# Two 128x128 turns moved from TensorE to VectorE and DRAM, taps in other places, the last block by token half

## The chip, the cores and the metric

One core of a Trainium2 chip runs the whole program. The metric is device time in microseconds (us). The kernel before took 2549.4 us, the median of three runs (2548.04 to 2549.49).

## The reference

Two transformer-like blocks over 256 tokens of width 2048, all in float32. What matters here:

```python
# first block, feed-forward (D_FF = 5632)
f = (silu(h @ w_ffn_gate) * (h @ w_ffn_up)) @ w_ffn_down

# second block, mixer: 2048 + 2*4*128 = 3072 convolved channels
proj = rmsnorm(h) @ w_in                  # z, xbc, dt_raw, q, k, v
xbc  = silu(causal_dwconv(xbc, conv_w, conv_b))   # width 4, along the tokens
# then a state-space scan over xbc and dt, gated by z, and
# attention in a window of 128 tokens over q, k, v; both into w_out

# second block, feed-forward, with a causal convolution of width 3 before the gate
# last: h + sigmoid(rmsnorm(h) @ w_ple_gate) * rmsnorm(p @ w_ple_proj)
```

## The kernel before

**Products.** Float32 operands are split into a high part (float32r, by ACT, line 781) and a low part (the rest, by VectorE, line 2157), and every product is three TensorE passes: high x high, high x low, low x high (lines 1475 to 1477, in `tokens`). A phase (`up1`, `down1`, `w_in2`, `up2`, `ple_gate` and so on) is a row of blocks of 512 output columns. A block streams its weights from DRAM in tiles of 512 rows (four slots of `raw`, by SP, `load_tile`); each tile is two halves (four slots of `w_hi` and of `w_lo`). With 2048 inputs a block has eight halves. A weight half may be split only when TensorE has used the half four before it; ACT and VectorE run three halves ahead (`LEAD = 3`). So in the loops of ACT and VectorE the place n of a block stands beside TensorE's half n, and splits half n + 3. What else ACT, VectorE and TensorE have to do is put at places by hand, after the split of that place (TensorE: after the half). Each engine runs its own list in order; semaphores join them.

**Tokens and channels.** Products come out with tokens on the partitions, in the PSUM banks `pair[:, b % 2]`, two blocks in turn. What is needed with channels on the partitions has to be turned.

- *First feed-forward* (`up1`, 22 blocks, half of the columns from the gate, half from the up matrix): at the end of block b ACT takes the SiLU of the gate half (`finish_up1`, line 1123) and VectorE multiplies by the up half into `ff_u` (`product`, line 2610). Beside half 3 of the next block TensorE turns the 2 x 2 squares of 128 x 128 into the PSUM tile `misc` (`turn_hidden`, line 1794), ACT copies them to `hid_hi` (line 1128), VectorE subtracts for `hid_lo` (line 2616). `down1` starts with the last of these. During the first blocks VectorE also sums modulation rows (line 2377), whose 512 KB tiles POOL loads.
- *Convolved channels* (`w_in2`, blocks 6 to 11 of 16, six blocks of 512 channels, `B_XBC` to `B_Z`): at the end of a block ACT evicts it, scaled by the norm, to `xbc_t` (line 1170). Beside half 0 of the next block TensorE turns it back into the bank it came from (`turn_xbc`, eight transposes, line 1950). At place 1 ACT writes the tap of the newest token with the bias into `xbc` (`conv_bias`, line 936, four instructions), and VectorE adds the three older taps, four instructions each, two at each of the places 1 to 6 (`conv_taps`, line 2318). TensorE's next block but one writes the same bank: it waits at its start for all twelve (`pe.wait_ge(c2_tap, 12 * (j - 1))`). The first z block turns the sixth.
- *Attention beside it*: from place 4 of the first convolved block one of 16 pairs of heads every two places. TensorE: values and scores after an even half (lines 1877, 1856, 1857), transposes of the probabilities after an odd one (line 1868). VectorE at each odd place: mask and maxima of one pair (lines 2748 to 2761), inverses and scaling of the pair before (lines 2764 to 2775). ACT: exponentials at even places (lines 1196, 1200), copies at odd ones (1208 before the split, 1233 after it). VectorE's `attention_beside` calls `attention(place)` and then `convolution(place)`.
- *Second feed-forward* (`up2`): the turn goes another way already. ACT evicts with the columns permuted into `ff_t`; SP writes it to DRAM (`keep_up2`) and reads it back (`back_up2`), so that what belongs to one 128 x 128 square is spread over the partitions such that VectorE's turn of 32 x 32 squares (`turn_up2`, line 3001) finishes it, into `misc`, at place 3.

**The end.** `ple_gate` has four blocks. After the last, ACT takes the sigmoid of each token half (line 1439), VectorE multiplies and adds (lines 3053, 3058), and SP stores each half.

Of the kernel before, what the change touches and what calls it, by code (L numbers as in the profile page):

```python
# [87 lines left out]
def two_blocks(nc, d, out):  # L88
# [125 lines left out]
    with ExitStack() as ctx:  # L214
# [84 lines left out]
        ff_u = at("ff_u", F + 90, [P, 2, S])  # L299
        ff_t = at("ff_t", R, [P, 4, T, P])  # L300
# [21 lines left out]
        xbc_t = at("xbc_t", F + 88, [P, T, COLS])  # L322
# [81 lines left out]
        def columns(tile, widths):  # L404
# [40 lines left out]
        ff_sig, ff_prod, ff_turned, h_hi, h_lo, c3_bias, c3_tap, up2_ev, up2_kept, up2_back, up2_turned = (  # L445
            sem(n) for n in ("ff_sig", "ff_prod", "ff_turned", "h_hi", "h_lo", "c3_bias", "c3_tap", "up2_ev", "up2_kept", "up2_back",
                             "up2_turned"))
        qkv_ev, dt_acc, dt_ev, xbc_turned, dt_hi, dt_lo, dt_mm, dt_x, dt_exp, hn_v, hn_s, k_ready, q_ready, qk_turned, qk_ev = (
            sem(n) for n in ("qkv_ev", "dt_acc", "dt_ev", "xbc_turned", "dt_hi", "dt_lo", "dt_mm", "dt_x", "dt_exp", "hn_v", "hn_s", "k_ready", "q_ready",
# [38 lines left out]
        TURN3_AT, CONV3_AT, SILU3_AT = 3, 4, 6  # L488


        TURN_XBC_AT, CONV2_AT, SILU2_AT, LATE_AT = 0, 1, 3, 4
# [30 lines left out]

        end_in, dt_raw, res_ready = sem("end_in"), sem("dt_raw"), sem("res_ready")
# [78 lines left out]
        def _(sp):  # L602
# [85 lines left out]

            def load_up1(b):
                load(up1, b, twin(d["w_ffn_gate"][0], b * (COLS // 2), d["w_ffn_up"][0], b * (COLS // 2)))  # L690
# [9 lines left out]
            load_all(down1, d["w_ffn_down"][0])  # L700
# [4 lines left out]
            for b in range(1, w_in2.blocks):  # L705
                if b == 2:
                    load_late()
                load(w_in2, b, plain(d["w_in_2"][0], bass.ds(w_in2_cols[b], COLS)))
            for b in range(w_out2.blocks):
                load(w_out2, b, plain(d["w_out_2"][0], bass.ds(b * COLS, COLS)))  # L710
            def keep_up2(b):

                sp.wait_ge(up2_ev, b + 1)
                if not isinstance(b, int) or b:
                    sp.wait_ge(up2_back, b * 16)
                sp.dma_start(up2_rows.rearrange("g p n -> p g n"), ff_t.rearrange("p g t q -> p g (t q)")).then_inc(up2_kept, 16)

            def back_up2(b):

                sp.wait_ge(up2_kept, b * 16 + 16)  # L720
                if not isinstance(b, int) or b:
                    sp.wait_ge(up2_turned, b)
                sp.dma_start(ff_back.rearrange("p i t q -> p (i t q)"),
                             up2_rows.rearrange("g (a i) n -> (g a) (i n)", i=4)).then_inc(up2_back, 16)

            def load_up2(b, turn):
                for j in range(up2.tiles):
                    load_tile(up2, b, j, twin(d["w_up_2"][0], b * (COLS // 2), d["w_up_2"][0], b * (COLS // 2) + HC * P))
                    if turn and j == 0:
                        keep_up2(b - 2)  # L730
                    elif turn and j == 1:
                        back_up2(b - 2)
# [5 lines left out]
            for j in range(down2.tiles):  # L738
                load_tile(down2, 0, j, plain(d["w_down_2"][0], bass.ds(0, COLS)))
                if j in (0, up2.tiles):  # L740
                    keep_up2(up2.blocks - 2 + j // up2.tiles)
                elif j in (1, up2.tiles + 1):
                    back_up2(up2.blocks - 2 + j // up2.tiles)
# [24 lines left out]
        def _(act):  # L768
# [298 lines left out]
            def gate2_out():  # L1067

                act.wait_ge(gt_row, XB + 1)
                act.wait_ge(res_ready, XB)  # L1070
                done(run(gt[0:KC, 0:P], misc[0:KC, 2, 0:P], ACT.Copy))
                done.wait()
                act.dma_start(by_chunk(gate_row_kept[0]), gt[0:KC, 0:P]).then_inc(row_ready, 16)
# [42 lines left out]
            def finish_up1(b, c):  # L1116

                if isinstance(b, int) and b == 8:
                    act.wait_ge(ple_landed, PLE_STORED)
                    mod_out(MOD_SUMS.index(9) + 1, JOINT_USED + 1, misc[:, 3, :], rows_late)  # L1120
                if not isinstance(b, int) or b:
                    act.wait_ge(ff_prod, b)
                run(ff_g[:], pair[:, c, :, GATE], ACT.Silu).then_inc(ff_sig, 1)

            def hidden_high(b, c):

                act.wait_ge(ff_turned, b)
                run(flat(hid_hi[:, bass.ds(b * 2 - 2, 2), :]), misc[:, c, :], ACT.Copy).then_inc(h_hi, 1)

            stream(up1, finish_up1, down1, peel=5, evict=hidden_high)  # L1130
            def beside_down1(b, place):
                if b:
                    norm2_beside(b - 1, place)
                elif place == LAST_HIDDEN + 1:
# [123 lines left out]
            for b in range(B_XBC, B_Z):  # L1258
                j = b - B_XBC
                mixer2(b, attention_beside, output)  # L1260
                if j:
                    act.wait_ge(xbc_turned, j)
                evict(xbc_t, b % 2).then_inc(qkv_ev, 1)
# [96 lines left out]
            def conv3_bias(b, c):  # L1360

                act.wait_ge(up2_turned, b)
# [25 lines left out]
            def finish_up2(b, c):  # L1388
# [3 lines left out]
                else:  # L1392
                    act.wait_ge(up2_kept, b * 16)
# [25 lines left out]
            for b in range(ple_gate.blocks):  # L1419
# [13 lines left out]
                act.wait_ge(w_used, ple_gate.end(b))  # L1433
# [4 lines left out]
                for t in range(T):  # L1438
                    ins = run(sig[:, t, :], pair[:, b % 2, t, :], ACT.Sigmoid, scale=scale[:, t:t + 1])
# [5 lines left out]
        def _(pe):  # L1445
# [340 lines left out]
            def turn_hidden(b, c):  # L1786

                pe.wait_ge(ff_prod, b)
                if not isinstance(b, int) or b > 2:

                    pe.wait_ge(h_lo, b - 2)
                for e in range(2):
                    for t in range(T):
                        mm = pe.transpose(misc[:, c, e * S + t * P:e * S + (t + 1) * P], ff_u[:, t, e * P:(e + 1) * P], ident[:])
                mm.then_inc(ff_turned, 1)

            def up1_block(b, c):

                def beside(h):
                    if h == 3 and (not isinstance(b, int) or b):  # L1800
                        turn_hidden(b, 1 - c)
# [24 lines left out]
            def last_hidden_turned(h):  # L1826
                if h == 0:
                    gate2_turn()
                elif h == LAST_HIDDEN:
                    turn_hidden(up1.blocks, 1)  # L1830
# [114 lines left out]
            def turn_xbc(j):  # L1945

                pe.wait_ge(qkv_ev, B_XBC + j)
                for m in range(4):
                    for t in range(T):
                        mm = pe.transpose(pair[:, (B_XBC + j - 1) % 2, m // 2, m % 2 * S + t * P:m % 2 * S + (t + 1) * P],  # L1950
                                          xbc_t[:, t, m * P:(m + 1) * P], ident[:])
                mm.then_inc(xbc_turned, 1)


            for b in range(B_XBC, B_Z):
# [6 lines left out]
                def beside(h):  # L1962
                    if j and h == TURN_XBC_AT:
                        turn_xbc(j)
# [77 lines left out]
            for b in range(B_Z, w_in2.blocks):  # L2042
# [6 lines left out]
                def beside(h):  # L2049
                    if j == 0 and h == TURN_XBC_AT:  # L2050
                        turn_xbc(B_Z - B_XBC)
# [89 lines left out]
            for b in range(ple_gate.blocks):  # L2141
                if b >= 2:
                    pe.wait_ge(gate_sig, b - 1)
                tokens(ple_gate, b, b % 2, normed, embedding if b == 0 else None, normed_yet(4) if b == 0 else None)


        @block.vector
        def _(dve):
# [13 lines left out]
            def stream(ph, finish, nxt, mod_pairs=0, beside=None, evict=None, paced=None):  # L2162
# [12 lines left out]
                def one(b, c, more, mods=False):  # L2175
# [6 lines left out]
                    if not (mods and b == 0):  # L2182
                        split_lo(ph, b, range(ph.lead, ph.halves), beside)
# [420 lines left out]
            def product(b, c):  # L2604

                dve.wait_ge(ff_sig, b + 1)
                if not isinstance(b, int) or b:

                    dve.wait_ge(ff_turned, b)
                dve.tensor_tensor(ff_u[:], ff_g[:], pair[:, c, :, UP], ALU.mult).then_inc(ff_prod, 1)  # L2610
# [8 lines left out]
            stream(up1, product, down1, mod_pairs=4, evict=hidden_low)  # L2619
# [24 lines left out]
            def beside_down1(b, place):  # L2644
                if b:
                    norm2_beside(b - 1, place)
                elif place == LAST_HIDDEN + 1:
                    hidden_low(up1.blocks, 1)
# [198 lines left out]

            def convolution(place):
# [149 lines left out]
            def turn_up2(b, c):  # L2998

                dve.wait_ge(up2_back, b * 16)  # L3000
                dve.transpose(misc[:, 2 * c:2 * c + 2, :].rearrange("p k (e t a i) -> p i t (k e) a", e=2, t=T, i=4),
                              ff_back.rearrange("p i t (m q) -> p i t m q", m=4)).then_inc(up2_turned, 1)
# [103 lines left out]
```

## Time and profile before

| | |
|---|---|
| median of three runs | 2549.4 us |
| the profiled execution | 2547.73 us, span 2546.0 us |
| TensorE busy | 2512.1 us (99%) |
| VectorE busy | 1608.0 us (63%) |
| ACT busy | 1255.5 us (49%) |
| first feed-forward's up blocks | from about 394 to 871 us |
| convolved channels | from about 1240 to 1425 us |
| granted TensorE clock | 0.998 of full |

Times in rows are from the span's start. A timeline row is start, duration, engine, line, operation, output and inputs, count of merged instructions, and in brackets the idle time before it and what ended that. An instruction of TensorE or VectorE overlaps the next one a little, so the distance of two starts tells more of what it costs than its duration.

### The profile page before, as it was taken

The page shows a single profiled execution, that of the slowest core. Times are in us where ns is not written, and L with a number is a line of the kernel's source. Part 1 is how long each engine was busy: PE and PEld are TensorE (multiplying, and loading weights), DVE is VectorE, ACT ScalarE, POOL GpSimd, SP SyncE. Part 2 cuts the span into 40 slices and gives each one's busy share as a digit, 9 for nine tenths or more (in the row PEclk, how much of TensorE's full clock was granted, in tenths as well). Part 3 has the DMA queues.
Part 4 walks back from the last instruction along what each step waited for, and adds up shares of the span by engine and source line. Part 5 has one row for each costly group of instructions (what it writes and reads, how often), then busy time and mean ns, then how long its engine had stood idle before and what let it go on. Part 6 is the DMA issues. An engine that isn't in the chain of part 4 may idle for free.

```text
span 2546.0 us, 32176 instructions
## 1 busy us (share of the span) xinstructions
PE 2512.1 (99%) x12226; PEld 2047.7 (80%) x12226; DVE 1608.0 (63%) x1958; ACT 1255.5 (49%) x1665; POOL 78.6 (3%) x165
## 2 busy tenths in 40 slices
PE   7999999999999999999999999999999999999999
PEld 1688878888888888888888888888888888888887
DVE  1468997764444455565888678446777777744445
ACT  2354454444444444454566656445555555544463
POOL 0012110100000000000000000000000000000000
PEclk9999999999999999999999999999999999999999
DMA  9999998865555556575534555566777777755564
GB/s 385 392 347 388 356 338 286 294 232 188 186 194 182 193 187 198 187 220 167 181 118 134 178 201 166 183 197 217 245 244 239 240 238 237 234 193 184 192 231 132
DMA packets 367708, 579.37 MB, mean 228 GB/s; under 512 B 19520, under 2 KB 213088, under 8 KB 367088
## 3 DMA queue, kind: packets, MB, share of 16 engines
q1 hardware_dynamic: 347088, 504.68, 59.5%
q0 software_dynamic: 19616, 71.34, 7.5%
q10 hardware_dynamic: 896, 1.84, 0.3%
q8 instruction: 75, 1.23, 0.2%
q14 instruction: 33, 0.27, 0.0%
HBM read 563.36 MB, written 14.46 MB: 227 GB/s over the span
## 4 chain that ended last, share of the span: by engine, by line
PE 93%; DMA 3%; DVE 2%; ACT 1%; issue 1%; SPq 0%; POOL 0%; DVEq 0%; ACTq 0%
PE pair L1475 28%; PE pair L1477 27%; PE pair L1476 27%; DMA mod_raw<-in_w_ada 2%; PE pair L1457 1%; PE pair L1458 1%; PE pair L1459 1%; PE misc L1628 1%; DVE w_lo L2157 1%; PE misc L2039 1%; PE misc L1491 1%; PE misc L1877 1%; DMA mod_page<-in_w_ada 0%; PE misc L1868 0%; PE misc L1856 0%
## 5 line engine op out<-in xcount | busy, mean ns | idle before, releaser
L2157 DVE TENSOR_TENSOR w_lo<-raw,w_hi 128x1024 fp32r<-128x1024 f32 x848 | 1015.6, 1203 | 786.0 <-ACT w_hi L781 783.4
L781 ACT ACTIVATE w_hi<-raw 128x1024 fp32r<-128x1024 f32 x848 | 882.4, 1043 | 982.9 <-PE pair L1477 906.6
L1475 PE MATMUL pair<-w_hi,a_hi 128*128 128x512 f32 x2048 | 805.6, 393 | 0.9 <-DVE w_lo L2157 0.7
L1477 PE MATMUL pair<-w_hi,a_lo 128*128 128x512 f32 x2048 | 797.8, 390 | 0.0
L1476 PE MATMUL pair<-w_lo,a_hi 128*128 128x512 f32 x2048 | 797.1, 389 | 0.0
L1475 PEld LDWEIGHTS pair<-w_hi,a_hi 128*128 128x128 f32 x2048 | 384.5, 188 | 83.6 <-issue 2.9
L1477 PEld LDWEIGHTS pair<-w_hi,a_lo 128*128 128x128 f32 x2048 | 384.4, 188 | 81.0
L1476 PEld LDWEIGHTS pair<-w_lo,a_hi 128*128 128x128 f32 x2048 | 384.7, 188 | 77.8 <-issue 0.5
L1475 PE MATMUL pair<-w_hi,hid_hi 128*128 128x512 f32 x704 | 274.6, 390 | 0.0
L1477 PE MATMUL pair<-w_hi,hid_lo 128*128 128x512 f32 x704 | 274.0, 389 | 0.0
L1476 PE MATMUL pair<-w_lo,hid_hi 128*128 128x512 f32 x704 | 273.9, 389 | 0.0
L1477 PEld LDWEIGHTS pair<-w_hi,hid_lo 128*128 128x128 f32 x704 | 132.2, 188 | 27.5
L1475 PEld LDWEIGHTS pair<-w_hi,hid_hi 128*128 128x128 f32 x704 | 132.2, 188 | 27.4
L1476 PEld LDWEIGHTS pair<-w_lo,hid_hi 128*128 128x128 f32 x704 | 132.2, 188 | 27.2
L1457 PE MATMUL pair<-a_hi,w_hi 128*128 128x256 f32 x384 | 111.6, 291 | 1.3 <-DVE xc L2318 1.0
L1458 PE MATMUL pair<-a_lo,w_hi 128*128 128x256 f32 x384 | 108.5, 283 | 0.0
L1459 PE MATMUL pair<-a_hi,w_lo 128*128 128x256 f32 x384 | 108.5, 283 | 0.0
L1457 PEld LDWEIGHTS pair<-a_hi,w_hi 128*128 128x128 f32 x384 | 73.4, 191 | 17.7 <-issue 13.1
L2377 DVE SCALAR_TENSOR_TENSOR mod_acc<-mod_raw,keep,mod_acc 128x1024 f32<-128x1024 f32 x60 | 76.7, 1279 | 10.4 <-DMA mod_raw<-in_w_ada 9.4
L1458 PEld LDWEIGHTS pair<-a_lo,w_hi 128*128 128x128 f32 x384 | 73.6, 192 | 0.1
L1459 PEld LDWEIGHTS pair<-a_hi,w_lo 128*128 128x128 f32 x384 | 73.5, 191 | 0.0
L580 POOL DMA_DIRECT2D mod_raw<-in_w_ada x86 | 45.6, 531 | 337.1 <-DVE mod_acc L2377 146.0
(392 smaller groups left out, 2119.4 us busy)
## 6 DMA issues: line engine op xcount, KB each, us to landing
raw<-in_w_in SPq DMA_DIRECT2D x88, 1024.0 KB, 5.4
raw<-in_w_up SPq DMA_DIRECT2D x176, 512.0 KB, 4.4
raw<-in_w_out SPq DMA_DIRECT2D x48, 1024.0 KB, 5.2
raw<-in_w_ffn_gate SPq DMA_DIRECT2D x88, 512.0 KB, 3.7
raw<-in_w_ffn_up SPq DMA_DIRECT2D x88, 512.0 KB, 4.6
mod_raw<-in_w_ada POOLq DMA_DIRECT2D x86, 512.0 KB, 7.2
raw<-in_w_ffn_down SPq DMA_DIRECT2D x32, 1024.0 KB, 5.0
raw<-in_w_down SPq DMA_DIRECT2D x32, 1024.0 KB, 5.1
```

The costliest lines, as they stand in the source:

```text
L580: pool.dma_start(mod_slot(n), ada[:, k, bass.ds(a * MOD_COLS, MOD_COLS)]).then_inc(page_landed[mod_landing(n)[0]], 16)
L781: run(w_hi[:, h % HALF_SLOTS, 0:n, :], raw[:, h // 2 % RAW_SLOTS, at0:at0 + n, :], ACT.Copy).then_inc(hi_ready, 1)
L1457: pe.matmul(o, wh, hi[:, k, :], start=(kh == kk == 0 and m % 2 == 0), stop=False, skip_group_check=True)
L1458: pe.matmul(o, wh, lo[:, k, :], start=False, stop=False, skip_group_check=True)
L1459: mm = pe.matmul(o, wl, hi[:, k, :], start=False, stop=(kh == ph.halves - 1 and kk == n - 1), skip_group_check=True)
L1475: pe.matmul(o, hi[:, own], w_hi[:, slot, kk, :], start=(h == kk == 0), stop=False)
L1476: pe.matmul(o, hi[:, own], w_lo[:, slot, kk, :], start=False, stop=False)
L1477: mm = pe.matmul(o, lo[:, own], w_hi[:, slot, kk, :], start=False, stop=(h == ph.halves - 1 and kk == n - 1))
L1491: mm = pe.transpose(misc[:, m % 4 // 2, m % 2 * S + t * P:m % 2 * S + (t + 1) * P], src[:, t, m * P:(m + 1) * P], ident[:])
L1628: mm = pe.matmul(bank[own], c_silu[:, k:k + 1].to_broadcast([P, P // 4]), tile[:, e * COLS:(e + 1) * COLS], start=(k < 2), stop=(k >= KC - ...
L2157: dve.tensor_tensor(w_lo[:, slot, 0:n, :], raw[:, h // 2 % RAW_SLOTS, at0:at0 + n, :], w_hi[:, slot, 0:n, :].bitcast(F32), ALU.subtract).t ...
L2377: dve.scalar_tensor_tensor(out=acc, in0=of, scalar=by, in1=acc, op0=ALU.mult, op1=ALU.add).then_inc(mod_step, 1)
```

## The change

1. *First feed-forward.* `product` writes `ff_parts`, its columns permuted, in place of `ff_u`. SP stores it to DRAM (`keep_up1`, after the first weight tile of the block after next) and reads it back (`back_up1`, after the second). VectorE turns squares of 32 x 32 into `misc` between the low halves 6 and 7 (`turn_hidden`); TensorE's `turn_hidden` is gone. ACT's SiLU, which writes where the read-back lands, waits for that turn. In `down1` the last turn is at place 3, the high and low copies one place later.
2. *Convolved channels.* The same by `keep_xbc`, `back_xbc` (two reads, one for each token half) and two VectorE turns at place 3. ACT's bias step is at place 3, the taps are three at each of places 4 to 7, the SiLUs of the sixth block at places 4 to 7. TensorE's `turn_xbc` is gone.
3. *Last block.* TensorE finishes token half 0 of the last gate block before it does the last four weight halves of token half 1; ACT's first sigmoid waits for the first only.
4. The three turns by DRAM share their semaphores, counted on.

```diff
+            def keep_up1(b):
+                sp.wait_ge(ff_prod, b + 1)
+                if not isinstance(b, int) or b:
+                    sp.wait_ge(parts_back, b * 16)
+                sp.dma_start(ff_rows.rearrange("g p n -> p g n"),
+                             ff_parts.rearrange("p g t q -> p g (t q)")).then_inc(parts_kept, 16)
+            def back_up1(b):
+                sp.wait_ge(parts_kept, b * 16 + 16)
+                sp.dma_start(ff_parts_back.rearrange("p i t q -> p (i t q)"),
+                             ff_rows.rearrange("g (a i) n -> (g a) (i n)", i=4)).then_inc(parts_back, 16)
...
+            def keep_xbc(j):
+                sp.wait_ge(qkv_ev, B_XBC + j + 1)
+                sp.wait_ge(parts_back, 16 * (XBC_TURNS + 2 * j))
+                sp.dma_start(xbc_rows.rearrange("g p n -> p g n"), xbc_t.rearrange("p g t q -> p g (t q)")).then_inc(parts_kept, 16)
+            def back_xbc(j):
+                sp.wait_ge(parts_kept, 16 * (XBC_TURNS + j + 1))
+                sp.wait_ge(parts_turned, XBC_TURNS + j)
+                for t in range(T):
+                    sp.dma_start(xbc_back[t][:], xbc_rows.rearrange("g (a i) (t q) -> t (g a) i q", i=4, t=T)[t]).then_inc(parts_back, 16)
...
-        TURN_XBC_AT, CONV2_AT, SILU2_AT, LATE_AT = 0, 1, 3, 4
+        TURN_XBC_AT, TAPS_XBC, SILU2_AT, LATE_AT = 3, {4: (0, 1, 2), 5: (3, 4, 5), 6: (6, 7, 8), 7: (9, 10, 11)}, 4, 4
... (ACT)
-                if j and place % w_in2.halves == CONV2_AT:
-                    act.wait_ge(xbc_turned, j)
+                if j and place % w_in2.halves == TURN_XBC_AT:
+                    act.wait_ge(parts_turned, XBC_TURNS + j)
                     conv_bias((B_XBC + j - 1) % 2, 4 * j - 4, cw2[:, (CONV - 1) * XBC:], cb2, xbc, c2_bias)
...
-                    act.wait_ge(ff_prod, b)
+                    act.wait_ge(parts_turned, b)
                 run(ff_g[:], pair[:, c, :, GATE], ACT.Silu).then_inc(ff_sig, 1)
... (VectorE)
-                        split_lo(ph, b, range(ph.lead, ph.halves), beside)
+                        split_lo(ph, b, range(ph.lead, ph.halves - 1), beside)
+                        turn(b, 1 - c)
+                        split_lo(ph, b, range(ph.halves - 1, ph.halves), beside)
...
+            def turn_hidden(b, c):
+                dve.wait_ge(parts_back, b * 16)
+                dve.transpose(misc[:, c, :].rearrange("p (m t a i) -> p i t m a", m=2, t=T, i=4),
+                              ff_parts_back.rearrange("p i t (m q) -> p i t m q", m=2)).then_inc(parts_turned, 1)
...
             def convolution(place):
                 j = place // w_in2.halves - 1
-                if j >= 0 and place % w_in2.halves >= CONV2_AT:
-                    conv_taps(place % w_in2.halves - CONV2_AT, (B_XBC + j) % 2, 4 * j, cw2, CONV, XBC, xbc, c2_bias, c2_tap, 12 * j)
+                c = (B_XBC + j) % 2
+                if j >= 0 and place % w_in2.halves == TURN_XBC_AT:
+                    dve.wait_ge(parts_back, 16 * (XBC_TURNS + 2 * j + T))
+                    for t in range(T):
+                        ins = dve.transpose(pair[:, c].rearrange("p k (e t a i) -> p t i (k e) a", e=2, t=T, i=4)[:, t],
+                                            xbc_back[t].rearrange("p i (m q) -> p i m q", m=4))
+                    ins.then_inc(parts_turned, 1)
+                for n in TAPS_XBC.get(place % w_in2.halves, ()) if j >= 0 else ():
+                    xbc_tap(n // 4 + 1, n % 4, c, 4 * j, 12 * j)
... (TensorE, last block)
+            for h in range(ple_gate.halves):
+                pe.wait_ge(lo_ready, ple_gate.half(ple_gate.blocks - 1) + h + 1)
+                mm = last_product(h, 0)
+                if h < ple_gate.halves - HALF_SLOTS:
+                    last_product(h, 1).then_inc(w_used, 1)
+            mm.then_inc(last_half, 1)
+            for h in range(ple_gate.halves - HALF_SLOTS, ple_gate.halves):
+                last_product(h, 1).then_inc(w_used, 1)
```

## Rows read from the trace of the kernel before

**Rows 1.** The page: busy time by engine, and the chain that ended last.

```profile
PE 2512.1 (99%) x12226; PEld 2047.7 (80%) x12226; DVE 1608.0 (63%) x1958; ACT 1255.5 (49%) x1665; POOL 78.6 (3%) x165
...
PE 93%; DMA 3%; DVE 2%; ACT 1%; issue 1%; SPq 0%; POOL 0%; DVEq 0%; ACTq 0%
```

**Rows 2.** TensorE's waits: line, releaser, us in total, times, longest us.

```profile
PE pair L1475 <- DVE w_lo L2157: 1.7, 3, 0.7
```

**Rows 3.** Busy us (and instructions) by stretch; then clock, DMA share, GB/s.

```profile
1304.30:1337.20 32.90, 32.90 (x210) 26.40 (x209) 28.63 (x61) 22.46 (x58) 0.00 (x0) 1.00 0.41 128
416.00:460.00 44.00, 44.00 (x199) 36.44 (x198) 33.06 (x30) 18.45 (x20) 5.29 (x10) 1.00 0.90 294
592.00:636.00 44.00, 44.00 (x200) 36.42 (x199) 21.71 (x21) 18.91 (x20) 0.00 (x0) 1.00 0.60 191
```

**Rows 4.** Timeline of TensorE around the turn in the first feed-forward.

```profile
650.70 0.60 PE L1794 MATMUL misc<-ident,ff_u 128*128 128x128 f32 x4
651.05 0.48 PE L1475 MATMUL pair<-w_hi,a_hi 128*128 128x512 f32 x1
...
651.84 0.39 PE L1475 MATMUL pair<-w_hi,a_hi 128*128 128x512 f32 x1
```

**Rows 5.** The turn of the second feed-forward: VectorE, read-back; write.

```profile
L3001 DVE STREAM_TRANSPOSE misc<-ff_back x22: 1252/1260/1262, 1755.4 to 2213.2; 128x1024 f32<-128x1024 f32 x22
...
DMA to landing us min/median/max: 5.4/5.7/7.1
...
up_rows<-ff_t SPq DMA_DIRECT2D x22, 512.0 KB, 2.9
```

**Rows 6.** Timeline of TensorE at a block's start among the convolved channels.

```profile
1336.68 0.82 PE L1868 MATMUL misc<-ident,scores 128*128 128x128 f32 x6
1337.25 0.48 PE L1475 MATMUL pair<-w_hi,a_hi 128*128 128x512 f32 x1
...
1340.07 1.04 PE L1950 MATMUL pair<-ident,xbc_t 128*128 128x128 f32 x8
1341.04 0.88 PE L1877 MATMUL misc<-p_tr,v_t 128*64 128x128 f32 x12
...
1342.71 0.50 PE L1475 MATMUL pair<-w_hi,a_hi 128*128 128x512 f32 x1
```

**Rows 7.** Timeline of VectorE over that block's start and after it.

```profile
1334.75 0.86 DVE L2318 SCALAR_TENSOR_TENSOR xbc<-pair,vec,xbc 128x253 f32<-128x253 f32 x2
1335.54 1.21 DVE L2157 TENSOR_TENSOR w_lo<-raw,w_hi 128x1024 fp32r<-128x1024 f32 x1
1336.67 0.94 DVE L2748 SCALAR_TENSOR_TENSOR scores<-misc,a_mask 128x768 f32<-128x768 f32 x1
...
1340.53 1.22 DVE L2157 TENSOR_TENSOR w_lo<-raw,w_hi 128x1024 fp32r<-128x1024 f32 x1
...
1344.66 0.95 DVE L2748 SCALAR_TENSOR_TENSOR scores<-misc,a_mask 128x768 f32<-128x768 f32 x1
...
1361.92 0.95 DVE L2748 SCALAR_TENSOR_TENSOR scores<-misc,a_mask 128x768 f32<-128x768 f32 x1
```

**Rows 8.** Timeline of ACT in the same block.

```profile
1340.32 0.21 ACT L1196 ACTIVATE page<-page 128x4 f32<-128x4 f32 x1
...
1342.17 0.37 ACT L1208 ACTIVATE o_f<-misc 128x256 f32<-128x256 f32 x1
...
1347.12 1.93 ACT L936 ACTIVATE xbc<-pair,vec 128x256 f32<-128x256 f32 x4
1348.92 1.07 ACT L781 ACTIVATE w_hi<-raw 128x1024 fp32r<-128x1024 f32 x1
```

**Rows 9.** Timeline of VectorE in the first z block.

```profile
1442.89 2.28 DVE L2878 TENSOR_TENSOR xdt<-xs_t,keep 128x2048 f32<-128x2048 f32 x1
```

**Rows 10.** Timeline of the last microseconds, ACT and VectorE.

```profile
2540.09 1.26 ACT L1439 ACTIVATE sig<-pair,keep 128x512 f32<-128x512 f32 x2 [9.81 <-PE pair L1477]
...
2542.86 0.69 DVE L3058 TENSOR_TENSOR x_res<-x_res,sig 128x512 f32<-128x512 f32 x1
```

More of the change, by code:

```diff
@@ L707, in _ @@
                     load_late()
-                load(w_in2, b, plain(d["w_in_2"][0], bass.ds(w_in2_cols[b], COLS)))
+                j = b - B_XBC - 2
+                for n in range(w_in2.tiles):
+                    load_tile(w_in2, b, n, plain(d["w_in_2"][0], bass.ds(w_in2_cols[b], COLS)))
+                    if 0 <= j < XBC // 4 and n == 0:
+                        keep_xbc(j)
+                    elif 0 <= j < XBC // 4 and n == 1:
+                        back_xbc(j)
             for b in range(w_out2.blocks):
@@ L1070, in gate2_out @@
                 act.wait_ge(res_ready, XB)
+                act.wait_ge(parts_kept, up1.blocks * 16)
                 done(run(gt[0:KC, 0:P], misc[0:KC, 2, 0:P], ACT.Copy))
@@ L1432, in _ @@
                         root(ROOT_PLE)
-                act.wait_ge(w_used, ple_gate.end(b))
+                if b == ple_gate.blocks - 1:
+                    act.wait_ge(last_half, 1)
+                else:
+                    act.wait_ge(w_used, ple_gate.end(b))
                 if b:
@@ L1438, in _ @@
                 for t in range(T):
+                    if t and b == ple_gate.blocks - 1:
+                        act.wait_ge(w_used, ple_gate.end(b))
                     ins = run(sig[:, t, :], pair[:, b % 2, t, :], ACT.Sigmoid, scale=scale[:, t:t + 1])
@@ L1943, in _ @@
             pe.wait_ge(dt_x, 1)
[L1945 to L1952, printed above, removed]
             for b in range(B_XBC, B_Z):
@@ L2139, in embedding @@
                     mm.then_inc(pe_mm, 1)
-            for b in range(ple_gate.blocks):
+            for b in range(ple_gate.blocks - 1):
                 if b >= 2:
@@ L2144, in _, with last_product @@
                 tokens(ple_gate, b, b % 2, normed, embedding if b == 0 else None, normed_yet(4) if b == 0 else None)
+            def last_product(h, t):
+                b = ple_gate.blocks - 1
+                slot, own = h % HALF_SLOTS, slice(t * P, (t + 1) * P)
+                _, k0, n = ple_gate.half_rows(h)
+                for kk in range(n):
+                    o, first, last = pair[:, b % 2, t, :], h == kk == 0, h == ple_gate.halves - 1 and kk == n - 1
+                    pe.matmul(o, a_hi[:, k0 + kk, own], w_hi[:, slot, kk, :], start=first, stop=False)
+                    pe.matmul(o, a_hi[:, k0 + kk, own], w_lo[:, slot, kk, :], start=False, stop=False)
+                    mm = pe.matmul(o, a_lo[:, k0 + kk, own], w_hi[:, slot, kk, :], start=False, stop=last)
+                return mm
+            pe.wait_ge(gate_sig, ple_gate.blocks - 2)
+            for h in range(ple_gate.halves):
[6 more added lines that the diff above has]
+                last_product(h, 1).then_inc(w_used, 1)
         @block.vector
@@ L2617, in hidden_low @@
                                   ALU.subtract).then_inc(h_lo, 1)
-            stream(up1, product, down1, mod_pairs=4, evict=hidden_low)
+            stream(up1, product, down1, mod_pairs=4, evict=hidden_low, turn=turn_hidden)
             def add_final(b, c):
@@ L2647, in beside_down1 @@
                 elif place == LAST_HIDDEN + 1:
+                    turn_hidden(up1.blocks, 1)
+                elif place == LAST_HIDDEN + 2:
                     hidden_low(up1.blocks, 1)
```

107 lines of the change are left out of this document (60 added, 47 removed).

## The prediction

> **What bounds the kernel now.** I read the page first: TensorE is busy 99% of a 2546.0 us span and holds 93% of the chain that ended last [rows 1]. So time is won by taking instructions off TensorE and lost wherever it has to wait. Next, the list of what TensorE waited for: weights from DRAM at the very start, and after that hardly anything; low weight halves cost it 1.7 us in three waits [rows 2]. Then the busy time by stretch, where the reader is to see two things [rows 3]. TensorE is busy 44.00 of 44 us and 32.90 of 32.90 in the stretches that the change touches. And VectorE has room in one and hardly any in the other: in the first feed-forward it is busy 21.71 of 44 us (33.06 in its first seven blocks, where the modulation rows are still summed), in a block of the convolved channels 28.63 of 32.90. Last the timelines of all engines over one block of each kind, which give the order in which that room is used.
>
> The kernel before ran 2547.73 us in the profiled execution, 1.73 us outside its span; the median of the runs shown is 2549.4 us. I work out a difference against the profiled execution and add it to the median.
>
> **Part 1, first feed-forward: 88 transposes leave TensorE.** Each of 22 blocks has four. They start at 650.70, the next product at 651.05, and the fourth product from there at 651.84, where a pitch of 0.227 us without transposes would have it at 651.38 [rows 4] (0.227 is 21.8 us by 96 products, the spacing of 22 turns from 1755.4 to 2213.2 where nothing stands between [rows 5]): four cost 0.46 us, with rounding 0.47 (TensorE's instructions overlap, so their 0.27 us each is not added up). 22 x 0.47 = **-10.4 us**. In their place SP writes and reads 256 KB per block and VectorE turns 512 elements per partition. The second feed-forward does this already with twice the bytes: the write lands after 2.9 us, the read after 5.7 (7.1 at most), the turn of 1024 elements takes 1.26 us [rows 5], so 0.64 for 512. It stands in the same place there, behind low half 6. The product ends 1.6 us into the block, so the data are back at 1.6 + 0.4 + 2.9 + 0.4 + 5.7 = 11 us, about when VectorE comes to the turn; low half 7, queued behind it, is wanted by TensorE at 19. Cost nothing: VectorE's idle half hides it. On SP the new write waits for the product in front of the second weight tile of a block, whose slot is freed only by a low half that VectorE does after that product, so it delays nothing; the read stands in front of the third. ACT's SiLU now waits for the turn and the product for the landed write, both 5 us old by then; the copy of the gate row at the start of the down projection waits for the last write, and comes three weight halves (8 us) after the product that it stores. What no row shows is the first seven blocks, with DMA engines at 90% and VectorE at 75% [rows 3]. A gain is excluded, since TensorE has no idle time to win; a loss reaches 8 us (1 us per block, transfers twice as long as in [rows 5]). I take 0, as in the nearest rows.
>
> **Part 2, convolved channels: 48 transposes leave, and VectorE gets late.** Eight stand from 1340.07 to 1341.04 [rows 6]: 0.97 us, six times, the last 0.87: -5.7 us. Now the price. Three edits meet in one block of eight places (one place per weight half): VectorE has two turns at place 3; the twelve taps, now two per place at places 1 to 6, become three per place at 4 to 7; ACT's bias step moves from place 1 to 3 and waits for the turn, in front of high half 7. The PSUM bank that the taps read is the one TensorE writes from the start of the next block, and its wait for all twelve is unchanged. At every odd place VectorE does the softmax of a head pair **before** its taps. At place 7 that ran from 1336.67 to 1340.53 [rows 7], while TensorE had begun the next block at 1337.25 [rows 6]. It could, because the last taps had ended at 1335.54, in place 6. Taps behind that softmax can't be done by 1337.25.
>
> How late, I get by walking the three queues in program order through a block. VectorE: low half 1.13 us to the next start, softmax 3.86 (4.0 with gaps), tap 0.39 [rows 7]. ACT: exponentials 1.85, output copy 0.3, four biases 1.8, high half 0.96 [rows 8]. TensorE: half 2.82, values and scores 1.67, probabilities' transposes 0.57 [rows 6], 8.0 us per two places. For the kernel before the walk puts two mask steps at 7.4 and 24.7 us of the block; the trace has 7.41 and 24.67 (1344.66 and 1361.92, less 1337.25) [rows 6, 7]. With the change, in steady state, S = 0 the start of a block: half 2 ends at 10.7; output copy and high half 6 till 13.0; low half 14.2; softmax 18.2; two turns of 0.64, whose bytes landed long before, 19.5; ACT's biases 21.4 and only then high half 7, 22.4; low half 23.6; three taps 24.8; meanwhile ACT's exponentials, copy and high half 8, 25.5; low half 26.7; softmax 30.7; taps 31.8; low half and taps 34.1; low half 35.3; softmax 39.3; taps 40.4. TensorE is through at 32 and starts the next block at **40.5, before 32.95**. VectorE's work adds up to only 30.5 us; not the sum but the order does it: it idles in places 0 to 2, waiting for weight halves, and the moved work comes at the end. Three blocks have a softmax at place 7 with taps behind it: 3 x 7.6 = +22.8 us, their transposes already off.
>
> The others by the same walk: the fourth, with softmaxes till place 5, 33.9 for 31.2, +2.7; the fifth, with none but four SiLUs in a row on ACT behind the biases, 25.2 for 23.9, +1.3; the first z block, where two multiplications of 2.28 us stand among the taps [rows 9], 32.1 for 27.7, +4.4. Behind that the state's operand, a third such multiplication, comes later for TensorE: between 0 and 2, I take +1. Part 2: 22.8 + 2.7 + 1.3 + 4.4 + 1 = **+32.2 us**. Bounds: a turn of 0.5 or 0.8 us instead of 0.64 moves six blocks by 0.3 each, -2 to +2; a read-back of 8 us adds 1.4 in the fifth block, where the turn could start at 11.8, nothing where it comes at 18. SP's share as in part 1: its write waits for the eviction, 2.3 us into a block, its weight tiles for later low halves. If nothing were queued up before place 7, each softmax block would still have, from the end of half 6, copy and high half 2.65, low half 1.2, softmax 4.0, taps 1.2 against 5.15 on TensorE: 3.9 us. So at the least 3 x 3.9 - 2.9 + 9.4 = +18.
>
> **Part 3, the end.** TensorE's work in the last block stays; token half 0's sigmoid, product and sum leave the tail. Before, the sigmoids start at 2540.09 and VectorE's last sum ends at 2543.55 [rows 10]. After, sigmoid 0.7, product 0.7, sum 0.7: 2542.2. **-1.3 us**, between -0.5 and -2.
>
> **Sum.** -10.4 + 32.2 - 1.3 = +20.5: span 2566.5, this execution 2568.2, median 2549.4 + 20.5 = **2569.9 us**.
>
> A rule of the Trainium skill speaks against parts 1 and 2 alike: "VectorE: DVE Perf Modes", Rules for kernel authors, leaves a 128x128 transpose to TensorE where a PSUM destination will do. TensorE's price here is 0.12 us each [rows 4, 6]. By the rule part 1 would bring nothing either, and the sum be +30.9; VectorE's idle half there [rows 3] is why I keep -10.4.
>
> **Rivals.**
> A, the forecast: late taps hold TensorE at six block starts. 2570, its own range 2562 to 2578. Chance 0.78.
> B, the other side: TensorE isn't held, because VectorE gets through place 7 in time. Then only savings count: -10.4 - 5.7 - 1.3 = -17.4, 2532 us. It decides whether the softmax at place 7 ends 1.2 us before TensorE's next block; against it, it ended 3.3 us after [rows 6, 7]; for it only that VectorE's sum, 30.5, is under TensorE's 32. 0.06.
> C: VectorE and ACT come early to place 7, with 3.9 us per softmax block and half of the other terms: 3 x 3.9 - 2.9 + 4.7 - 11.7 = +1.8, 2551. Against it, that the walk fits the trace. 0.07.
> D: A, and in the first feed-forward the read-back comes too late, so that low half 7 waits behind the turn and TensorE for it, 0.47 us a block: the saving is gone, 2549.4 + 30.9 = 2580. For it, DMA engines at 90% in the first seven blocks; against it, 60% later [rows 3]. 0.09. The rule of the Trainium skill above would end here too.
>
> **Range and chances.** A whole, and what lies between it and D: 2560 to 2580, with 0.2 outside. Less than 0.2% (5 us) this kernel's measurement can't tell from no change. Slower: A, D and 0.02 of C = 0.89; same: the rest of C, 0.04; faster 0.07.
>
> **What would show it.** Right: TensorE idle at the start of six blocks from the third convolved one on, released by the line of the taps, three times by 7 to 9 us; block pitch 40.5; VectorE going softmax, three taps, next low half; blocks of the first feed-forward 21.8 us long, before 22.2, without a wait; the last sum done 2.1 us after its sigmoid starts. Wrong: a pitch of 32 in the convolved blocks (B) or one of about 36 (C); waits for low halves in the first feed-forward (D).

## The result: slower by 1.2%, and the profile after

The changed kernel takes 2578.35 us (2577.26 to 2578.48, four runs); the kernel before took 2548.78 in the same session. Ratio 1.0115, 95% interval 1.0100 to 1.0130: 29.6 us more, where the prediction had 20.5 more. The profiled execution took 2578.43 us with a span of 2576.7.

On the page, TensorE is as busy as before in microseconds, though it issues 136 instructions fewer, and its share of the chain that ended last has fallen from 93 to 86%; VectorE's rose from 2 to 6% [rows 1].

```profile
PE 2510.4 (97%) x12090; PEld 2042.3 (79%) x12090; DVE 1628.5 (63%) x1992; ACT 1256.5 (49%) x1665; POOL 78.9 (3%) x165
...
PE 86%; DVE 6%; DMA 3%; ACT 3%; issue 1%; SPq 0%; POOL 0%; ACTq 0%; DVEq 0%
```

TensorE's waits, as in [rows 2] (line, releaser, us in total, times, longest). The line of the taps is new and holds 29.6 us; the low halves hold what they held. Waits for the taps' line begin six blocks, as forecast. The second row is the transposes of the probabilities, late once in each of four blocks. The profile names no releaser for them. In the kernel they wait for ACT's copy of an attention output (line 1258), and each of the four waits ends 0.09 to 0.11 us after that copy. It stands on ACT behind the biases, high half 7 and the exponentials.

```profile
PE pair L1533 <- DVE xbc L2916: 29.6, 6, 6.8
...
PE misc L1911 <- issue: 5.2, 4, 1.9
...
PE pair L1533 <- DVE w_lo L2209: 1.6, 3, 0.7
```

```profile
1328.80 0.38 ACT L1258 ACTIVATE o_f<-misc 128x256 f32<-128x256 f32 x1
...
1329.27 0.84 PE L1911 MATMUL misc<-ident,scores 128*128 128x128 f32 x6 [1.02 <-issue]
```

VectorE's timeline over the start of the block that begins at 1344.95 (start, us, what it does), against [rows 7]: the last softmax (1339.77 to 1343.7), then three taps, then the next block's low half. In the kernel before the same softmax stood over TensorE's start too, but no tap came behind it.

```profile
1338.64 1.21 DVE L2209 TENSOR_TENSOR w_lo<-raw,w_hi 128x1024 fp32r<-128x1024 f32 x1
1339.77 0.95 DVE L2811 SCALAR_TENSOR_TENSOR scores<-misc,a_mask 128x768 f32<-128x768 f32 x1
...
1342.70 1.03 DVE L2838 TENSOR_TENSOR scores<-scores,page 128x512 f32<-128x512 f32 x2
1343.64 1.25 DVE L2916 SCALAR_TENSOR_TENSOR xbc<-pair,vec,xbc 128x253 f32<-128x253 f32 x3
1344.81 1.21 DVE L2209 TENSOR_TENSOR w_lo<-raw,w_hi 128x1024 fp32r<-128x1024 f32 x1
```

TensorE over the same start, against [rows 6]. A wait was forecast here, of 8.5 us by the walk (40.5 less the 32 at which TensorE is through) and 7 to 9 by its signs; it is 6.78, with another 1.02 us inside the block before the transposes just named. Look at what comes behind it: the products start 0.43 us apart (1345.54, 1345.97, 1346.39), where the warm pitch is 0.23.

```profile
1337.35 0.82 PE L1911 MATMUL misc<-ident,scores 128*128 128x128 f32 x6
1344.95 0.80 PE L1533 MATMUL pair<-w_hi,a_hi 128*128 128x512 f32 x1 [6.78 <-DVE xbc L2916]
1345.54 0.63 PE L1534 MATMUL pair<-w_lo,a_hi 128*128 128x512 f32 x1
1345.97 0.63 PE L1535 MATMUL pair<-w_hi,a_lo 128*128 128x512 f32 x1
1346.39 0.63 PE L1533 MATMUL pair<-w_hi,a_hi 128*128 128x512 f32 x1
```

The busy time by stretch has the reason in its third column from the end, the granted clock (1.00 is 2.4 GHz, 0.50 is 1.2). Full before the wait, it is 0.67 on the mean while TensorE stands idle, 0.50 in the first four microseconds of the block, and 1.00 again behind them. In the first row of [rows 3] it was 1.00 throughout.

```profile
1331.50:1338.00 6.50, 6.50 (x45) 5.02 (x43) 6.29 (x16) 3.60 (x12) 0.00 (x0) 1.00 0.21 80
1338.50:1344.50 6.00, 0.00 (x0) 0.00 (x0) 5.80 (x15) 4.58 (x13) 0.00 (x0) 0.67 0.84 262
1345.00:1349.00 4.00, 4.00 (x10) 3.14 (x11) 1.03 (x1) 0.00 (x0) 0.00 (x0) 0.50 0.46 101
1352.00:1356.00 4.00, 4.00 (x26) 3.27 (x23) 3.11 (x4) 0.86 (x2) 0.00 (x0) 1.00 0.11 26
```

The six starts, by TensorE's timeline; "12 products" is the time from the first to the twelfth product of the block, 2.63 at full clock:

| block starts at | wait before | 12 products | pitch to next start | forecast |
|---|---|---|---|---|
| 1302.90 | 6.80 | 4.28 | 42.05 | 40.5 |
| 1344.95 | 6.78 | 4.86 | 43.06 | 40.5 |
| 1388.01 | 6.77 | 4.37 | 35.70 | 33.9 |
| 1423.71 | 1.25 | 2.63 | 26.48 | 25.2 |
| 1450.19 | 3.38 | 4.02 | 33.01 | 32.1 |
| 1483.20 | 4.65 | 4.54 | | |

Part 1 has two rows, VectorE's turns and the landing of their read-back in the first feed-forward; the next two are the same for part 2. Last, the end, against [rows 10]: one product and one sum behind the last sigmoid. From the start of that sigmoid to the end of the last sum it is 2.13 us; before, two sigmoids stood there, and from the start of the first it was 3.46.

```profile
L2670 DVE STREAM_TRANSPOSE misc<-ff_parts_back x22: 718/720/728, 408.3 to 864.4; 128x512 f32<-128x512 f32 x22
...
DMA to landing us min/median/max: 4.4/4.8/6.8
...
L2928 DVE STREAM_TRANSPOSE pair<-xbc_back x12: 683/702/721, 1280.8 to 1464.8; 128x512 f32<-128x512 f32 x12
...
DMA to landing us min/median/max: 5.7/6.0/6.6
...
2572.09 0.69 ACT L1497 ACTIVATE sig<-pair,keep 128x512 f32<-128x512 f32 x1 [4.75 <-PE pair L2185]
2572.81 0.69 DVE L3133 TENSOR_TENSOR sig<-sig,pe_t 128x512 f32<-128x512 f32 x1 [4.02 <-ACT sig L1497]
2573.53 0.69 DVE L3138 TENSOR_TENSOR x_res<-x_res,sig 128x512 f32<-128x512 f32 x1
```

### The profile page after: what moved, and what is told of

Read it like the earlier page. It is cut to its first block, busy times and chain, and to the rows that moved or that the text cites. A ratio compares the mean times of both kernels' runs of the same rounds, so it can differ in the third digit from the quotient of the medians.

```text
span 2576.7 us, 31988 instructions
## 1 busy us (share of the span) xinstructions
PE 2510.4 (97%) x12090; PEld 2042.3 (79%) x12090; DVE 1628.5 (63%) x1992; ACT 1256.5 (49%) x1665; POOL 78.9 (3%) x165
## 4 chain that ended last, share of the span: by engine, by line
PE 86%; DVE 6%; DMA 3%; ACT 3%; issue 1%; SPq 0%; POOL 0%; ACTq 0%; DVEq 0%
PE pair L1533 26%; PE pair L1534 26%; PE pair L1535 26%; DMA mod_raw<-in_w_ada 2%; DVE w_lo L2209 1%; PE pair L1515 1%; PE pair L1517 1%; PE pair L1516 1%; ACT w_hi L830 1%; PE misc L1686 1%; DVE xbc L2916 1%; ACT scores L1250 1%; PE misc L2071 1%; PE misc L1549 1%; DMA mod_page<-in_w_ada 0%
## 5 line engine op out<-in xcount | busy, mean ns | idle before, releaser
L1533 PE MATMUL pair<-w_hi,a_hi 128*128 128x512 f32 x2016 | 795.8, 395 | 30.5 <-DVE xbc L2916 29.6
L1535 PE MATMUL pair<-w_hi,a_lo 128*128 128x512 f32 x2016 | 788.3, 391 | 0.0
L1534 PE MATMUL pair<-w_lo,a_hi 128*128 128x512 f32 x2016 | 788.0, 391 | 0.0
L1515 PEld LDWEIGHTS pair<-a_hi,w_hi 128*128 128x128 f32 x384 | 74.1, 193 | 17.4 <-issue 13.1
```

The lines of the kernel that those rows point to most:

```text
L1515: pe.matmul(o, wh, hi[:, k, :], start=(kh == kk == 0 and m % 2 == 0), stop=False, skip_group_check=True)
L1533: pe.matmul(o, hi[:, own], w_hi[:, slot, kk, :], start=(h == kk == 0), stop=False)
L1534: pe.matmul(o, hi[:, own], w_lo[:, slot, kk, :], start=False, stop=False)
L1535: mm = pe.matmul(o, lo[:, own], w_hi[:, slot, kk, :], start=False, stop=(h == ph.halves - 1 and kk == n - 1))
```

## The experiments

**The parts apart.** The first kernel is the changed one with part 2 undone: turns of the convolved channels on TensorE (eight transposes a block, in `turn_xbc`), ACT's biases at place 1, two taps a place at 1 to 6, the SiLUs of the sixth block one place earlier.

```diff
-        TURN_XBC_AT, TAPS_XBC, SILU2_AT, LATE_AT = 3, {4: (0, 1, 2), 5: (3, 4, 5), 6: (6, 7, 8), 7: (9, 10, 11)}, 4, 4
+        TURN_XBC_AT, TAPS_XBC, SILU2_AT, LATE_AT = 1, {1: (0, 1), 2: (2, 3), 3: (4, 5), 4: (6, 7), 5: (8, 9), 6: (10, 11)}, 3, 4
...
+                    if j and h == 0:
+                        turn_xbc(j)
...
```

> The changed kernel with part 2 undone: the convolved channels are turned by TensorE beside half 0 again, biases at place 1, two taps per place at 1 to 6. Parts 1 and 3 stay. Theory (parts 1 and 3 save, part 2 costs everything): 2548.8 - 10.4 - 1.3 = 2537 us, TensorE without waits at the starts of the convolved blocks and its clock at full level throughout, so that part 2 is worth 2578.4 - 2537 = +41 us where I had forecast +32. Rival (part 1's turns do cost something, as the rule for VectorE has it, in the first seven blocks): 2540 to 2548 us, with waits of TensorE between 390 and 550 us.

Measured: 2537.31 us (2536.93 to 2537.91), before 2548.13, ratio 0.9957 [0.9940, 0.9973]. So part 2 costs 2578.35 - 2537.31 = 41.0 us, all of the loss and more; run a second time on another chip the kernel took 2536.37 (ratio 0.9955 [0.9938, 0.9971]). No wait for taps is left in its trace, and the clock is full through all blocks of the convolved channels.

The second is the kernel before with part 3 alone.

> The kernel before with part 3 alone, the last block by token half. Theory: 1.3 us less, 2547.5, the last sum ending 2.1 us after its sigmoid starts instead of 3.4. Rival (VectorE's two steps of the first token half weren't what the second waited for): no difference, 2548.8.

Measured: 2546.93 us (2545.95 to 2548.37, ten runs), ratio 0.9996 [0.9987, 1.0006]. The 1.2 us between the medians are what was forecast, but the interval holds zero: by time alone this part isn't shown, only by the rows of the tail above (this kernel's own trace has the same 2.13 us from the last sigmoid's start). The difference to the first experiment, 2537.31 - 2546.93 = -9.6 us, is part 1.

**The order at place 7.** If the wait stands because taps are queued behind a softmax, doing the taps first must shorten it by nearly that softmax.

```diff
             def attention_beside(place):
-                attention(place)
-                convolution(place)
+                if place % w_in2.halves == 7:
+                    convolution(place)
+                    attention(place)
+                else:
+                    attention(place)
+                    convolution(place)
```

> The changed kernel, with one order changed: at place 7 of a convolved block VectorE does its three taps before the softmax and not behind it. The same instructions. Theory (TensorE waits for taps queued behind a softmax): each of the three softmax blocks loses 4 us of its wait, the walk gives 35.9 to 36.7 us of pitch for 40 to 40.6, so 12 us less, and 1 to 5 us more from shorter stretches at the lower clock: 2562 to 2566. Rival (VectorE simply has too much to do, wherever it stands): no difference, 2578, as the three taps then delay the softmax and with it the probabilities and the scores.

Measured: 2565.91 us (2563.77 to 2566.53), 12.4 less than the changed kernel; ratio to before 1.0068 [1.0051, 1.0085]. The three long waits fell from 6.8 to 2.9 us each, the other three stayed. The pitches of the softmax blocks fell to 39.31 and 38.09 us; the walk gave 35.9 to 36.7, and left the slow clock to be added:

```profile
PE pair L1533 <- DVE xbc L2916: 18.1, 6, 4.7
```

VectorE's timeline, before the second of these starts, has the taps ahead of the softmax:

```profile
1335.56 1.25 DVE L2916 SCALAR_TENSOR_TENSOR xbc<-pair,vec,xbc 128x253 f32<-128x253 f32 x3
1336.73 0.95 DVE L2811 SCALAR_TENSOR_TENSOR scores<-misc,a_mask 128x768 f32<-128x768 f32 x1
```

But the clock stayed as bad: 12 products took 4.86, 4.05 and 4.21 us behind waits of 2.9, 13.1 us together for 13.5 behind waits of 6.8. TensorE's timeline shows how it goes: the first products come at the warm pitch, and from 1337.67 on they slow down, with the wait already over.

```profile
1336.87 0.50 PE L1533 MATMUL pair<-w_hi,a_hi 128*128 128x512 f32 x1 [2.91 <-DVE xbc L2916]
1337.20 0.40 PE L1534 MATMUL pair<-w_lo,a_hi 128*128 128x512 f32 x1
1337.44 0.39 PE L1535 MATMUL pair<-w_hi,a_lo 128*128 128x512 f32 x1
1337.67 0.46 PE L1533 MATMUL pair<-w_hi,a_hi 128*128 128x512 f32 x1
1337.93 0.63 PE L1534 MATMUL pair<-w_lo,a_hi 128*128 128x512 f32 x1
```

**The clock by itself.** The theory for the missing 9 us: waits cost a second time, by a slow start behind them. To test it the waits are kept and TensorE is kept working through them: 46 transposes, whose results nobody reads, ahead of its wait for the taps in the three softmax blocks.

```diff
                 else:
+                    if j <= 4:
+                        pe.wait_ge(p_ev, 4 * (j - 1))
+                        for _ in range(46):
+                            pe.transpose(misc[:, 2, 0:P], x[:, 0, 0:P], ident[:])
                     pe.wait_ge(c2_tap, 12 * (j - 1))
```

> The changed kernel plus 46 transposes of 128x128 on TensorE, results unused, before its wait for the taps in each of the three blocks where it idles 6.8 us (behind ACT's copy of the probabilities, whose bank they use). 46 x 0.12 = 5.5 us, which fit into the wait. Theory (what I missed, about 9 us, is the clock: the records show 1.2 GHz in stretches of 3 to 10 us that begin in those waits and reach behind them, products then at a pitch of 0.43 us instead of 0.23): the clock stays at 2.4 GHz at those three starts and the time falls by the 6 us that the slow stretches behind them cost, to 2572. Rival (the 9 us are VectorE's and ACT's, the turn of 0.71 us and longer steps, and the slow clock is hidden by the same waits): no gain, 2578 or a little more.

Measured: 2571.53 us (2570.02 to 2574.35), 6.8 less than the changed kernel though TensorE does more; ratio to before 1.0095 [1.0078, 1.0112]. The taps still release it (0.67 us after the filler), and the products behind are 0.23 to 0.24 us apart:

```profile
1336.10 5.24 PE L1997 MATMUL misc<-ident,x_res 128*128 128x128 f32 x46 [0.90 <-ACT p_tr L1283]
1342.02 0.50 PE L1533 MATMUL pair<-w_hi,a_hi 128*128 128x512 f32 x1 [0.67 <-DVE xbc L2920]
1342.36 0.40 PE L1534 MATMUL pair<-w_lo,a_hi 128*128 128x512 f32 x1
1342.60 0.40 PE L1535 MATMUL pair<-w_hi,a_lo 128*128 128x512 f32 x1
```

The granted clock over the first two of these blocks (third column from the end) was 0.92 and 0.87 in the changed kernel, and is 1.00 here:

```profile
1300.00:1340.00 40.00, 37.46 (x246) 30.11 (x244) 29.63 (x63) 22.38 (x58) 0.00 (x0) 1.00 0.42 129
1340.00:1380.00 40.00, 37.41 (x245) 30.03 (x244) 29.63 (x62) 22.34 (x58) 0.00 (x0) 1.00 0.42 128
```

From a block's first product to the first of its second half, the three blocks took 6.27, 7.28 and 6.35 us in the changed kernel and 4.62, 4.65 and 4.61 here: 1.65 + 2.63 + 1.74 = 6.0 us of the 6.8. Elsewhere slow stretches changed places: the start behind 3.36 us is not slow here (12 products in 2.67 us for 4.02), but inside the fourth block 12 products take 4.02 us that took 2.62. And the starts are now 40.39 and 40.42 us apart (1301.63, 1342.02, 1382.44), for a walk that gave 40.5.

**Which of the three edits in part 2 makes the wait?** The first kernel again, its turns left on TensorE and the biases at place 1, with only the taps at places 4 to 7.

```diff
-        TURN_XBC_AT, TAPS_XBC, SILU2_AT, LATE_AT = 1, {1: (0, 1), 2: (2, 3), 3: (4, 5), 4: (6, 7), 5: (8, 9), 6: (10, 11)}, 3, 4
+        TURN_XBC_AT, TAPS_XBC, SILU2_AT, LATE_AT = 1, {4: (0, 1, 2), 5: (3, 4, 5), 6: (6, 7, 8), 7: (9, 10, 11)}, 3, 4
```

> The kernel with part 2 undone (2537.3 us), with only the taps moved: TensorE turns beside half 0, biases at place 1, no turn on VectorE, but taps three each at places 4 to 7. Theory (it is the place of the taps that costs, not the turn): the walk gives pitches of 37.3 to 38.1 us for 31.8 to 32.6, and with the rest 20.6 us more than with taps at 1 to 6, plus about 5 us of slow clock: 2558 to 2563. Rival (the turn on VectorE and ACT's bias step behind it are the greater part): within 8 us of 2537.

Measured: 2562.35 us (2561.85 to 2564.75), ratio 1.0056 [1.0039, 1.0073]: 2562.35 - 2537.31 = 25.0 us for the places of the taps alone. TensorE waits for them six times again:

```profile
PE pair L1509 <- DVE xbc L2906: 17.2, 6, 4.7
```

The pitches are 40.8 and 40.9 us where the walk gave 37.3 to 38.1. Slow starts fill that gap: from a block's first product to its second half, eight transposes included, these blocks took 8.27 and 8.37 us, 5.46 in the first kernel. So the late taps are the larger half of part 2. What remains to 41.0 is the turn on VectorE with ACT's biases two places later and the SiLUs one, 16.0 us, although TensorE is rid of its 48 transposes.

**The turn early.** The changed kernel with turn and biases at place 2 and four taps each at places 3, 4 and 6, none at 7.

```diff
-        TURN_XBC_AT, TAPS_XBC, SILU2_AT, LATE_AT = 3, {4: (0, 1, 2), 5: (3, 4, 5), 6: (6, 7, 8), 7: (9, 10, 11)}, 4, 4
+        TURN_XBC_AT, TAPS_XBC, SILU2_AT, LATE_AT = 2, {3: (0, 1, 2, 3), 4: (4, 5, 6, 7), 6: (8, 9, 10, 11)}, 4, 4
```

> The changed kernel with other places: VectorE's turns and ACT's biases at place 2, where no softmax stands, taps four each at 3, 4 and 6, none at 5 and 7. The same instructions, TensorE without transposes for the convolved channels. Theory (places decide): the walk gives pitches of 35 us, not 32, as the chain from turn to biases to high half 7 still delays ACT, 25 us less than the changed kernel; and 5 to 7 us of slow clock less if the waits are short: 2546 to 2553, so still above 2537.3 with the turn on TensorE. Rival 1 (the DRAM way is ahead wherever VectorE can fit it): 2532, 5.7 us under 2537.3. Rival 2 (the read-back isn't there at place 2): VectorE waits for it, 2560 or more.

Measured: 2545.76 us (2544.60 to 2547.14, ten runs), ratio 0.9992 [0.9982, 1.0001]. The wait for taps is down to 2.8 us in five, each at most 1.5, and no block's start is at the 0.43 us pitch; but the pitch of the softmax blocks is 34.8 to 35.0 us, and the list of waits from 1262 to 1475 tells where to look. ACT stands at its biases until VectorE has turned, 17.8 us in six. The output copy queued behind them ends at 1312.52, and TensorE's transposes of the probabilities, which need it, start at 1312.62:

```profile
ACT xbc L985 <- DVE pair L2928: 17.8, 6, 4.8
...
PE misc L1911 <- issue: 5.1, 4, 1.4
```

**The biases one place behind the turn.** The same kernel with one more line changed, so that ACT doesn't stand at a turn that is about to be made.

```diff
-                if j and place % w_in2.halves == TURN_XBC_AT:
+                if j and place % w_in2.halves == TURN_XBC_AT + 1:
```

> e7 with one step moved: ACT's biases at place 3, behind its high half 6 and the probabilities' copy, where the turn of place 2 is already done; VectorE's turns at place 2, taps four each at 3, 4 and 6. Theory (what e7 still lost was ACT standing in front of its bias step, 17.8 us in six waits, with the probabilities' and output copies behind it for which TensorE waited 5.1 us): the walk gives pitches of 31.6 us and the whole saving of part 2's transposes, 5.7 us, at no price: 2537.3 - 5.7 = 2531.6 us, TensorE without waits among the convolved channels. Rival (the read-back, for which VectorE waited 5.0 us in e7, holds the turn and so everything behind it): about 2536 to 2546.

Measured: 2532.75 us (2531.64 to 2535.06), before 2547.88, ratio 0.9943 [0.9927, 0.9960]; the first experiment ran beside it at 2536.37. This kernel beats both, the first experiment by 3.6 us where 5.7 were expected. ACT's wait is 3.5 us in two, and VectorE meets the read-back before it has landed, 6.3 us in five (5.0 in the kernel before this one); that delays nothing of TensorE's in the two blocks below. TensorE has no gap left in a softmax block; one wait for taps stays, 0.9 us at the start of the first z block:

```profile
DVE pair L2928 <- DMA xbc_back<-xbc_rows: 6.3, 5, 2.5
...
ACT xbc L985 <- DVE pair L2928: 3.5, 2, 2.3
```

```profile
1293.65:1325.73 32.08, 32.08 (x201) 25.53 (x200) 30.41 (x64) 22.51 (x59) 0.00 (x0) 1.00 0.55 172
1325.73:1357.81 32.08, 32.08 (x201) 25.54 (x200) 29.07 (x62) 22.47 (x60) 0.00 (x0) 1.00 0.50 156
```

## Why the prediction was right, and by how much it missed

**Which way it goes, and through what: right.** The likeliest case, A, is what came: late taps hold TensorE at six block starts, and the changed order at place 7 confirms the queue behind it (12.4 us back for the three softmaxes moved).

**Part 1: right.** Forecast -10.4, measured -9.6 as the difference of two experiments. The later blocks are 21.76 us long (VectorE's turns start that far apart), forecast 21.8, and TensorE waits for no low half, so D falls and the waits for the read-back (7.9 us in five of the first blocks on VectorE) stay hidden. The turn takes 0.72 us, not the 0.64 halved from the longer one: half the elements cost 57% of the time. That size was off and decided nothing here. The rule weighed against it, "VectorE: DVE Perf Modes", Rules for kernel authors, in the Trainium skill, would have had part 1 bring nothing; the runs decide against it here.

**Part 2: the mechanism right, its size too small: +41.0 against +32.2.** The walk's order of work was right. Set against the first experiment, where nothing waits (its blocks start at 1263.72, 1295.78, 1328.73, 1361.67, 1392.90, 1416.67 and 1444.12), the changed kernel's pitches give the price of each block. The first of them starts at 1263.12 in the changed kernel; the other starts are in the table above.

| block | longer by | forecast |
|---|---|---|
| three with a softmax at place 7 | 7.7, 9.1, 10.1 | 7.6 each |
| fourth | 4.5 | 2.7 |
| fifth | 2.7 | 1.3 |
| first z block | 5.6 | 4.4 |
| behind the last start | 1.4 | 1 |

What failed in size is the term for the softmax blocks, the step "**40.5, before 32.95**": it took TensorE's first half of a block at its warm 2.82 us. Behind the wait it runs at half the clock. That lengthened three blocks, two of these and the fourth, by 1.65, 2.63 and 1.74 us against the kept-busy kernel, and their pitches missed the forecast by 1.55, 2.56 and 1.80; with the clock kept up, the pitch was 40.4. The start of a block is where the walk hangs everything, since half 2's end releases ACT and through it VectorE, so the delay isn't absorbed but arrives whole at the next start. These 6.0 of the 8.8 us missing are shown by experiment.

The rest is read from rows only. The first z block starts slowly too (12 products 1.39 us over 2.63) and is 1.2 us over its forecast. Behind the last start the 12 products are 1.91 us slower, yet only 1.4 us are lost in all, so nothing is to be seen of the 1 us forecast for the state's operand. The fifth block, 26.48 for 25.2, has no slow start. In it ACT loads an activation table before the first SiLU, 1.28 us that the walk doesn't name, and VectorE idles 0.93 us for the high half behind that SiLU:

```profile
1438.70 1.07 ACT L830 ACTIVATE w_hi<-raw 128x1024 fp32r<-128x1024 f32 x1
1439.79 1.28 ACT L1293 ACT_TABLE_LOAD   x1
1441.09 1.06 ACT L1293 ACTIVATE xbc<-xbc 128x1024 f32<-128x1024 f32 x1
...
1443.13 1.23 DVE L2209 TENSOR_TENSOR w_lo<-raw,w_hi 128x1024 fp32r<-128x1024 f32 x1 [0.93 <-ACT w_hi L830]
```

No run took that load away, so as the fifth block's cause it is likely, not shown. Over the five slow starts the 12 products took 8.9 us more than 2.63 each. That this is almost the whole miss is chance: the fifth block's 1.4 us, which are no matter of the clock, stand where the state's 1 us did not come.

The trace of before could not show this price among these blocks, since TensorE never idled there [rows 3]. The Trainium skill has the rule, "TensorE: Matmul & The Clock Gate", HAM oscillation: idle gaps let the clock fall and the next work starts cold. Every start behind 4.65 us or more in the changed kernel agrees, 0.43 us a product for 0.23. That a wait should be billed by its length and by a cold start was the missing term.

**Part 3: right in the trace** (2.1 us of tail), not separable by time.

**B and C.** B needs the taps out before the next block starts; moving them to places 3, 4 and 6 and the biases behind the turn makes nearly that. The kernel then takes 2532.75, which looks like B's 2532 but isn't quite: B had -17.4 from 2549.4, and this is 15.1 below the 2547.88 beside it. Its saving for part 2 was sized too large. Between 1258 and 1442 us this kernel gains 4.0 us on the first experiment run beside it, not 5.7: eight transposes cost TensorE 0.89 us and not 0.97 (5.46 us to a block's second half with them, 4.57 without), and 0.9 us of waiting is left. So the change missed most of these savings by where it put the work. C's sign, a pitch of about 36, didn't come in the changed kernel (42.05 and 43.06), and its premise, VectorE and ACT early at place 7, was tested by no run. Of C's chance of 0.07 the prediction counts 0.02 as slower and 0.04 as same, though it calls that the rest; 0.01 is left out there and stands under faster.

## What to carry to other kernels

Where one queue is in order, look at what stands **behind** the longest step of a slot, not at the sum of the work: VectorE had 1.5 us to spare in each block by the forecast's sum of its work and still held TensorE for 6.8; in the last kernel it is busy 30.41 and 29.07 of 32.08 us in two blocks and holds nothing up there. When the walk through the queues gives TensorE an idle stretch of some microseconds, add a slow start to the price, 1.4 to 2.6 us in the changed kernel and up to 2.9 where transposes follow, and carry that through the rest of the walk. Look also for table loads in ACT's queue. And put the consumer in another queue one slot behind its producer: one line was worth 13.0 us (2545.76 to 2532.75).

## What the runs showed of the hardware

How long TensorE waited does not by itself say whether the next products are slow. In the kept-busy kernel it waited 3.36 us before 1443.51 and stayed at full clock, but 1.87 us before 1407.13 was followed by 12 products in 4.02 us; the same 1.87 us before 1414.43 in the changed kernel was followed by 12 in 2.62. Against that stand 2.9 us in the taps-first kernel with 12 products at 4.05 to 4.86, and 1.25 us in the changed one at 2.63. Two waits of almost one length, 3.36 there and 3.38 in the changed kernel, came out on opposite sides, and the 2.94 us at 1297.56 in the taps-first kernel cost as slow a start (4.86) as the worst behind 6.8. The windows of the kept-busy kernel behind the two waits (granted clock third from the end):

```profile
1443.60:1446.50 2.90, 2.90 (x13) 2.31 (x14) 0.97 (x1) 1.89 (x2) 0.00 (x0) 1.00 0.84 307
1408.00:1411.00 3.00, 3.00 (x9) 2.38 (x8) 2.92 (x7) 1.75 (x2) 0.00 (x0) 0.51 0.85 304
```

What decides between them stays open. A turn on VectorE into PSUM does not halve with its elements: 0.70 to 0.72 us for 512 a partition against 1.26 for 1024 [rows 5].
